# Layer norms of a two-layer decoder trunk: square root and reciprocal in place of logarithm, exponential and a refining step

## What is computed

```
def _layer_norm(x, g, b):
    mu = jnp.mean(xf, axis=-1, keepdims=True)
    var = jnp.mean(jnp.square(xf - mu), axis=-1, keepdims=True)
    y = (xf - mu) * lax.rsqrt(var + LN_EPS)
    return (y * g + b).astype(x.dtype)

for l in range(DEPTH):
    ...mixer of layer l gives yp, ys
    xp = _layer_norm(ALPHA * xp + yp, ln1_g[l], ln1_b[l])
    ...
    fp, cp = _conv_ffn(xp, w_up[l], conv_w[l], conv_b[l], w_down[l], c0)
    xp = _layer_norm(ALPHA * xp + fp, ln2_g[l], ln2_b[l])
```

## Time and profile before

| | us |
|---|---|
| median of 3 runs | 1877.13 |
| lowest and highest run | 1874.84 and 1877.6 |
| the profiled execution | 1879.82 |
| its span in the profile | 1877.7 |

### The profile page before, as it was taken

The page is one execution under the profiler, slowest core; times in us unless marked ns, Lnnn a source line. Parts: engine busy times, 40 slices in busy tenths (PEclk is TensorE's granted clock), DMA queues, the critical chain, the costliest instruction groups (busy, mean ns, idle before and its releaser), DMA issues.

```text
span 1877.7 us, 33921 instructions
## 1 busy us (share of the span) xinstructions
PE 1770.1 (94%) x12962; PEld 1573.3 (84%) x12962; DVE 883.8 (47%) x1406; ACT 521.3 (28%) x737; POOL 143.6 (8%) x119
## 2 busy tenths in 40 slices
PE   8999899979999999979989989989987999999996
PEld 7877444869999999969669759859946999999995
DVE  3224665465552455352372263263257555245544
ACT  3122443142221222132222222222323322122213
POOL 0000000020000000024013013013011000000000
PEclk9988898989999999999999999999999999999999
DMA  8976688212232222213343333333332223222221
GB/s 280 338 239 227 224 266 291 92 34 89 83 105 74 84 89 94 85 34 102 107 157 98 118 137 104 126 134 101 140 123 67 74 87 106 77 86 82 94 97 47
DMA packets 84072, 234.43 MB, mean 125 GB/s; under 512 B 9633, under 2 KB 9794, under 8 KB 83506
## 3 DMA queue, kind: packets, MB, share of 16 engines
q1 hardware_dynamic: 83138, 228.26, 36.4%
q0 software_dynamic: 880, 5.49, 0.8%
HBM read 209.90 MB, written 23.80 MB: 124 GB/s over the span
## 4 chain that ended last, share of the span: by engine, by line
PE 87%; DVE 5%; DMA 3%; ACT 2%; issue 2%; SPq 1%; DVEq 0%; ACTq 0%
PE banks L1258 70%; PE banks L1482 2%; PE banks L1564 2%; PE banks L1389 2%; DMA w_raw<-in_w_in_ab 2%; PE banks L1556 2%; PE banks L1289 1%; PE banks L1430 1%; PE banks L1445 1%; PE banks L1544 1%; DVE x_lo L1031 1%; PE banks L1417 1%; SPq L296 1%; DVE y L1010 1%; DMA s<-in_s 1%
## 5 line engine op out<-in xcount | busy, mean ns | idle before, releaser
L1258 PE MATMUL banks<-x_hi,w_hi 128*128 128x272 f32 x2624 | 552.1, 292 | 36.9 <-DVE x_lo L1031 27.8
L1258 PE MATMUL banks<-x_hi,w_lo 128*128 128x272 f32 x2624 | 547.4, 290 | 0.0
L1258 PE MATMUL banks<-x_lo,w_hi 128*128 128x272 f32 x2624 | 546.1, 290 | 0.0
L669 DVE TENSOR_TENSOR w_lo<-w_raw,w_hi 128x1024 fp32r<-128x1024 f32 (+2 forms) x228 | 277.5, 1217 | 547.5 <-ACT w_hi L441 547.3
L441 ACT ACTIVATE w_hi<-w_raw 128x1024 fp32r<-128x1024 f32 (+2 forms) x228 | 238.3, 1045 | 1056.8 <-PE banks L1258 915.8
L1258 PEld LDWEIGHTS banks<-x_hi,w_hi 128*128 128x128 f32 x2624 | 416.8, 190 | 47.6 <-issue 25.8
L1258 PEld LDWEIGHTS banks<-x_lo,w_hi 128*128 128x128 f32 x2624 | 417.5, 191 | 0.0
L1258 PEld LDWEIGHTS banks<-x_hi,w_lo 128*128 128x128 f32 x2624 | 414.3, 191 | 0.0
L1258 PE MATMUL banks<-act_hi,w_lo 128*128 128x272 f32 x704 | 145.3, 287 | 0.0
L1258 PE MATMUL banks<-act_lo,w_hi 128*128 128x272 f32 x704 | 145.1, 287 | 0.0
L1258 PE MATMUL banks<-act_hi,w_hi 128*128 128x272 f32 x704 | 145.1, 287 | 0.0
(11 more groups left out here) (226 smaller groups left out, 1678.0 us busy)
## 6 DMA issues: line engine op xcount, KB each, us to landing
w_raw<-in_w_up SPq DMA_DIRECT2D x88, 512.0 KB, 3.5
kv<-in_kc SPq DMA_DIRECT2D x128, 256.0 KB, 4.4
kv<-in_vc SPq DMA_DIRECT2D x128, 256.0 KB, 4.2
w_raw<-in_w_rin SPq DMA_DIRECT2D x48, 512.0 KB, 3.5
w_raw<-in_w_dn SPq DMA_DIRECT2D x32, 704.0 KB, 4.0
s<-in_s SPq DMA_DIRECT2D x32, 512.0 KB, 7.0
out_ret_s<-s SPq DMA_DIRECT2D x32, 512.0 KB, 2.7
w_raw<-in_w_in_ab SPq DMA_DIRECT2D x20, 512.0 KB, 6.4
```

The costliest lines, as they stand in the source:

```text
L669: V.tensor_tensor(w_lo[:, j, 0:k * P], w_raw[:, j, 0:k * P], w_hi[:, j, 0:k * P].bitcast(F32), ALU.subtract).then_inc(lo_ready, 1)
L1258: last = mm(B[:, 2 * j + half, 0:HN], a[:, j, w], x[:, kt, half * HN:(half + 1) * HN], start=kt == 0 and n == 0, stop=kt == k - 1 and n == 2)
```

## The change

ScalarE's logarithm and exponential become one square root, with the same input, bias and output tile, and the table set that is loaded at L557 becomes the one with the square root. VectorE's three refining instructions become one reciprocal of std in place. The multiplication of the gains by -0.5 is removed; the wait ahead of it stays. The number of table loads and the order of all other instructions on all engines are as before.

```diff
             def norm(n):
-                nc.scalar.preload_act_table_set("natural_log_exp_and_others")
+                nc.scalar.preload_act_table_set("sqrt_and_others")
                 for m in range(KD):
...
                 act.wait_ge(sq_used, n * KD + KD)
-                step.add(nc.scalar.activation(halves(std[:, :]), B[:, 6:8, 0:HN], ACT.Ln, bias=eps))
-                step.wait()
-                nc.scalar.activation(std[:, :], std[:, :], ACT.Exp, scale=-0.5).then_inc(std_ready, 1)
+                nc.scalar.activation(halves(std[:, :]), B[:, 6:8, 0:HN], ACT.Sqrt, bias=eps).then_inc(std_ready, 1)
...
                     dve.wait_ge(const_in, 3 * 16)
-                    step.add(V.tensor_scalar(lnp[:, :, 0, :], lnp[:, :, 0, :], -0.5, None, ALU.mult))
...
                 dve.wait_ge(std_ready, n + 1)
-                step.add(V.tensor_tensor(s1[:, :], std[:, :], std[:, :], ALU.mult))
-                step.wait()
-                step.add(V.scalar_tensor_tensor(halves(s1[:, :]), B[:, 6:8, 0:HN], eps, halves(s1[:, :]),
-                                                ALU.add, ALU.mult))
-                step.wait()
-                step.add(V.scalar_tensor_tensor(std[:, :], s1[:, :], 3.0, std[:, :], ALU.subtract, ALU.mult))
+                step.add(V.reciprocal(std[:, :], std[:, :]))
                 step.wait()
                 dve.wait_ge(c_ready, (n + 1) * KD)
                 scale(0)
```

## The result

The changed kernel is slower by 0.3%: the ratio of its time to that of the kernel before is 1.003, with a 95% interval of 1.002 to 1.004, that is 3.8 to 7.5 us. In that comparison (14 runs of each) the medians were 1884.43 us (1879.92 to 1888.18) and 1878.33 us (1873.38 to 1883.77). In proportion to the 1877.13 us of the forecast this is 1882.8 us. The forecast was 1879.2, with 1875.5 to 1884.0 as its range. The range held. The likeliest case, no change within 0.2%, did not come, though the interval begins just there.

A forecast was written before the change was run, and what follows sets the result against it. TensorE bounds the kernel but waits in each norm for a ScalarE-VectorE chain; replacing 3.06 us there by 3.58 adds 0.52 us a norm, +2.1 us over four, taking 1877.13 to 1879.2 us, range 1875.5 to 1884.0.

The forecast's parts named there:

- The place: Logarithm to first scaling in each of four norms: TensorE waits, so every 0.1 us there is 0.1 us of kernel.
- The reciprocal's size: VectorE's new 128x544 reciprocal in each norm: 3520 ns, extrapolated at 6.2 ns an element from three small reciprocals.
- the prediction's other two slopes: Per-element price of VectorE's reciprocal from pairs of small ones: 6.0 ns gives 3415 ns, 7.0 ns gives 3954 ns.
- Rival 2: VectorE's reciprocal runs at the usual rate after a one-time filling, 725 ns: -9.1 us, 1868.0 us; chance 10%.
- Rival 1: VectorE's reciprocal is longer: 7 ns an element gives 1880.9 us, eight passes (8.3 ns) 1883.8 us; chance 27%.
- The square root, the table load, the gains: ScalarE's L565 and table load at L557, VectorE's gains multiplication at L800: exchange or removal worth nothing.
- The sum: End of L565 to first scaling: 3.58 us against 3.06, +0.52 us a norm, +2.1 us for four.
- the prediction's own sign: TensorE's gap before the first L1258 behind a norm grows from 6.41 to some 6.9 us, matching the changed rows.
- Rival 3: TensorE's clock drops in products behind the first two norms too, +2.4 us: 1881.6, or misses the third: 1878.0; chance 8%.
- "Within 0.2%": Whole kernel: time stays within 0.2%, or 3.75 us, of before, the main forecast of 1879.2 us; chance 55%.
- "slower": Whole kernel slower by over 0.2%, through a longer reciprocal or TensorE's clock behind the norm; chance 35%.
- the eight-pass reciprocal: VectorE's reciprocal at eight passes of 1.04 ns an element: 4664 ns, +6.6 us in all, 1883.8 us.

The follow-up runs named there:

- the second reciprocal: Changed kernel with useless TensorE products in all three places, plus another full reciprocal per norm into an unread tile: median 1893.64 us, ratio 1.0076 to the kernel before.
- the missing refining step: Kernel before without its refining step and the gains' factor: ratio 0.9936 to the kernel before, -12.0 us, median 1868.13 us.
- the second profiles: Both kernels run once more without an edit, against the kernel before: changed kernel ratio 1.0024, median 1881.54 us; kernel before ratio 1.0002.
- the pause: Kernel before plus a VectorE memset of a 128x544 scratch tile behind each norm's refining step: ratio 1.0039 to the kernel before, +7.3 us.
- the half reciprocal: Kernel before with refining step and gains' factor replaced by an unread 128x272 reciprocal, logarithm and exponential kept: ratio 1.0003 to the kernel before.
- the work behind the squares: Changed kernel plus eight calls of useless TensorE products behind the last square, none around the mean: ratio 1.0022 to the kernel before, median 1883.01 us.
- Idle work: Kernel before plus unread TensorE products ahead of the column sums' wait, behind the mean and behind the last square: ratio 0.9985 to the kernel before.

## Why the prediction was right, and where it was not

- **The place.** Right. All four norms pass their VectorE time on to the kernel, as the second reciprocal (+15.5 to +16.9 us for 14.4) and the missing refining step (-12.0 for -9.4) show from both sides.
- **The reciprocal's size.** Right: 3520 ns forecast, 3553 measured. The slope of 6.2 ns from three instructions of one, four and five elements held up to 544; the half size gives 6.25. That it came within 1% is partly luck: the prediction's other two slopes from the same rows, 6.0 and 7.0 ns, would have been 4% short and 11% long. Rival 2 (a filling, then the usual rate) is excluded by the 1853 ns of the half size. Rival 1's steeper slopes, 7.0 and 8.3 ns, are excluded too. The Trainium skill's repeat count of 8 (VectorE: DVE Perf Modes, "First, the fixed hardware budget") is not to be read as eight times an ordinary element: 6.25 ns is six times the 1.04 ns of the earlier trace rows.
- **The square root, the table load, the gains.** The first two right at nothing: 714 ns for 713, 1283 ns for 1283. No run takes the gains' multiplication out alone, so its price of nothing is not tested.
- **The sum.** +2.1 us on the path forecast, +2.25 measured, and by the prediction's own sign TensorE's gap grew as the changed rows did, by 0.56 us for 0.57. Yet the kernel lost 3.8 to 7.5 us. The step that failed is the one that took the path's sum for the kernel's. Rival 3 had the right resource, the clock, and the wrong place: it looked at the product behind the norm and gave +2.4 us more at 8%. In the changed kernel's first profile that did happen once, behind norm 1 (0.62 over 843 to 847 us), while the drop behind norm 2 that the earlier trace rows have for the kernel before did not come there (1.00 over 1464 to 1468 us). In the second profiles the kernel before had such a drop behind norms 0 and 2 (0.57 over 419 to 423 us and over 1460 to 1464) and the changed kernel had none. So the rows do not show that the longer standstill brings drops behind the norm. The larger part lay ahead of the reciprocal, in the squares' stage, +6.1 us between the two profiles. There the forecast read the timeline of norm 0 and saw only when the squares' product ended; it did not ask why that stage took 11.5 us there and 8.8 in the other three norms. The clock behind norms 1 and 2 of the changed kernel:

```profile
843.00:847.00 4.00, 4.00 (x23) 4.00 (x23) 0.65 (x3) 1.89 (x3) 2.47 (x4) 0.62 0.26 65
...
1464.00:1468.00 4.00, 3.90 (x31) 3.90 (x32) 1.75 (x4) 2.66 (x5) 2.47 (x3) 1.00 0.15 54
```

- **"Within 0.2%" at 55%.** Did not come; "slower" at 35% did. The slower cases had been put down mainly to a dearer reciprocal, and came by way of the clock. That the range held is luck in part: its upper end of 1884.0 was set by the eight-pass reciprocal, which is excluded, and the kernel got near it for another reason. The span of 1877.5 to 1880.8 given for slopes of 5.6 to 6.9 ns should begin at 1877.9.

**What stays open** is why the kernel before has short squares' stages in its norms 1 to 3 in both profiles, and the changed kernel in none. Neither the reciprocal (the pause without it has long ones) nor the length of the standstill (the half reciprocal has a shorter one, and long stages) decides it. Nor are the stages of the other kernels always long: in norms 1 to 3 the pause, the half reciprocal, the missing refining step and the work behind the squares had 7 long ones in 12. What those kernels share is that their norms begin at other times after one another than before. The Trainium skill (TensorE: Matmul & The Clock Gate, "Part 1: The HAM clock gate") says that the gate judges by recent activity in a rhythm of its own that does not restart with a kernel, and that the same kernel can meet it differently from run to run. That would make the kernel before a case of luck in its spacing. It fits the rows, and the first square as the place where the clock falls or does not; but the pause and the half reciprocal shifted the spacing only together with the standstill, no run shifted it alone, and so this is argued and not shown.

## What to carry to other kernels

Fewer instructions are not less time: on VectorE a reciprocal of 544 elements costs as much as five ordinary instructions of that size, so what stands between a sum and the next product should have its price read per element, from the smallest instances if need be. A slope from three tiny instructions was good to 1% over a hundredfold extrapolation here, but single pairs of them gave 6.0 and 7.0 ns; a run at half the size is what made it sure. And where an edit lies between short standstills of TensorE, compare the granted clock of the stages beside it: a change of 2 us on the path came with 2 to 3 us more there, and a few matmuls without use in the short waits take that part out.

## What was not expected

- Standstills of 1.65 and 1.50 us, with 1.2 us of matmuls between them, are enough for the clock to drop to 1.2 GHz in the stage behind: 21 of 32 such stages took 10.3 us or more instead of 8.8. With both filled down to 0.35 to 0.41 and 0.21 us, none of 24 did.
- Idle work made the kernel before faster: 0.9985 (0.9972 to 0.9997).
- Filling 3.6 of the 7 us behind the squares did nothing for the squares' stages and nothing measurable for the time.
- The reciprocal's 6.25 ns an element, from 272 and 544 elements, also gives the small ones within 3 ns: 159, 178 and 184 ns for one, four and five elements, where the earlier trace rows have 157, 178 and 181.
